# Two transformer blocks on one core: probability transposes in two pairs, and two feed-forward tiles on the un-normed stream

## What is computed

```python
    u = rmsnorm(h, ffn_norm_pre[l])
    gt = causal_dwconv(u @ ffn_w_gate[l], ffn_conv_w[l], ffn_conv_b[l])
    y = (jax.nn.gelu(gt, approximate=True) * (u @ ffn_w_up[l])) @ ffn_w_down[l]
    h = h + rmsnorm(y, ffn_norm_post[l])
```

```python
    logits = scores - slopes * dist.astype(jnp.float32)
    mx = jnp.maximum(logits.max(axis=-1, keepdims=True), sink)
    e = jnp.exp(logits - mx)
    p = e / (e.sum(axis=-1, keepdims=True) + jnp.exp(sink - mx))
    out = jnp.einsum('bkgnqs,bnskd->bnqkgd', p.astype(v.dtype), vv)
```

```python
    s = jnp.einsum('bhtd,bhsd->bhts', q, k) * jnp.exp(log_d - m_t[..., None])
    num = jnp.einsum('bhts,bhsd->bhtd', s, v) + a_inter[..., None] * jnp.einsum('bhtk,bhkv->bhtv', q, c_st)
    c_new = decay[..., None, None] * c_st + jnp.einsum('bhsk,bhsv->bhkv', k * w[..., None], v)
```

## Time and profile before

| | |
|---|---|
| median of 3 runs | 2849.12 us (2843.03 to 2854.50) |
| profiled execution | 2844.58 us, span 2842.8 us |
| granted TensorE clock, mean | 0.974 |
| busy: TensorE, VectorE, ScalarE, GpSimd | 94%, 68%, 45%, 25% |
| way in, way down, mixers | 757 to 1238, 1238 to 1466, 1751 to 1922 us |

### The profile page before, as it was taken

How to read it: one execution, slowest core, us unless ns; L and a number is a source line. 1 busy time by engine, 2 the same in 40 slices (tenths; PEclk the granted TensorE clock), 3 DMA queues, 4 the chain that set the end, 5 groups by cost and what they waited for, 6 DMA issues and landing times. The chain is left out here.

```text
span 2842.8 us, 38460 instructions
## 1 busy us (share of the span) xinstructions
PE 2667.1 (94%) x14346; PEld 2310.5 (81%) x14346; DVE 1919.3 (68%) x2417; ACT 1284.8 (45%) x1968; POOL 711.7 (25%) x446
## 2 busy tenths in 40 slices
PE   8989999999879999999989998889998999999993
PEld 7989999899768888878868887767785688888882
DVE  5366556363388777777884723766355899999996
ACT  4242332332343233234544204764332577777773
POOL 3000000002255555513620000005400244444441
PEclk9999999999989999999999999999998999999997
DMA  5342323343212222266742111114203799999996
GB/s 186 108 133 90 100 97 101 119 138 119 96 45 75 81 89 76 80 216 198 232 140 67 45 60 67 39 45 141 74 18 141 272 422 417 416 415 415 413 413 242
DMA packets 267201, 472.04 MB, mean 166 GB/s; under 512 B 24338, under 2 KB 183330, under 8 KB 241970
## 3 DMA queue, kind: packets, MB, share of 16 engines
q1 hardware_dynamic: 257554, 435.49, 42.8%
q0 software_dynamic: 9504, 34.61, 3.0%
HBM read 398.61 MB, written 71.43 MB: 165 GB/s over the span
## 5 line engine op out<-in xcount | busy, mean ns | idle before, releaser
L4084 DVE TENSOR_TENSOR k_w_lo<-k_raw,k_w_hi 128x2048 fp32r<-128x2048 f32 x192 | 433.4, 2287 | 34.6 <-ACT k_w_hi L4020 31.0
L4020 ACT CAST k_w_hi<-k_raw 128x2048 fp32r<-128x2048 f32 x192 | 363.2, 1912 | 64.3 <-PE bank L3938 41.3
L120 PE MATMUL bank<-u_hi,p_w_hi 128*128 128x342 f32 (+2 forms) x720 | 236.9, 329 | 8.9 <-DVEq L889 6.0
L121 PE MATMUL bank<-u_lo,p_w_hi 128*128 128x342 f32 (+2 forms) x720 | 231.1, 321 | 0.0
L122 PE MATMUL bank<-u_hi,p_w_lo 128*128 128x342 f32 (+2 forms) x720 | 230.8, 321 | 0.0
L3936 PE MATMUL bank<-k_w_hi,k_x_hi 128*128 128x512 f32 x512 | 203.0, 397 | 1.3 <-DVE k_x_lo L4090 1.0
L3938 PE MATMUL bank<-k_w_hi,k_x_lo 128*128 128x512 f32 x512 | 199.8, 390 | 0.0
L3937 PE MATMUL bank<-k_w_lo,k_x_hi 128*128 128x512 f32 x512 | 199.3, 389 | 0.0
L1467 PE MATMUL bank<-u_ffn_hi,f_w_hi 128*128 128x512 f32 (+3 forms) x520 | 170.7, 328 | 16.8 <-DVE f_inner L1757 8.4
L1468 PE MATMUL bank<-u_ffn_lo,f_w_hi 128*128 128x512 f32 (+3 forms) x520 | 167.2, 322 | 0.0
L1469 PE MATMUL bank<-u_ffn_hi,f_w_lo 128*128 128x512 f32 (+3 forms) x520 | 166.7, 321 | 0.0
(11 more groups left out here) (620 smaller groups left out, 7502.7 us busy)
## 6 DMA issues: line engine op xcount, KB each, us to landing
k_raw<-in_w_e_gate_dram SPq DMA_DIRECT2D x64, 1024.0 KB, 7.1
k_raw<-in_w_e_up_dram SPq DMA_DIRECT2D x64, 1024.0 KB, 7.7
k_raw<-in_w_e_down_dram SPq DMA_DIRECT2D x64, 1024.0 KB, 8.3
f_raw<-in_ffn_w_down_dram SPq DMA_DIRECT2D x77, 256.0 KB, 3.0
p_w<-in_w_in_dram SPq DMA_DIRECT2D x34, 512.0 KB, 4.4
f_raw<-inner_scratch SPq DMA_DIRECT2D x55, 256.0 KB, 3.5
f_raw<-in_ffn_w_gate_dram SPq DMA_DIRECT2D x22, 512.0 KB, 3.7
f_raw<-in_ffn_w_up_dram SPq DMA_DIRECT2D x22, 512.0 KB, 4.9
```

Source lines behind the costliest of these rows:

```text
L120: pe.matmul(out, wh[:, t, :], xh[t][:, c:c + n], start=t == 0, stop=False)
L121: pe.matmul(out, wh[:, t, :], xl[t][:, c:c + n], start=False, stop=False)
L4020: act.copy(wh[:, q, :], raw[:, r, :]).then_inc(hi_made, 1)
L4084: dve.tensor_tensor(wl[:, q, :], raw[:, r, :], wh[:, q, :], ALU.subtract).then_inc(lo_made, 1)
```

## The change

*Way in.* Tile 1 also runs on the un-normed stream, right behind tile 0, and its gate and its product are scaled by `token` afterwards; tile 2 is the first on the normed stream and takes its k steps as they come. VectorE makes all low parts of the normed stream and of the sums, GpSimd only those of the weights. Tile 3 becomes a plain tile by columns, and the tiles with seven products begin at 4. TensorE's wait for the first four low weights moves behind the first sums of squares.

```diff
-PLAIN = (0, 1, 2, KF - 1)
+PLAIN = (0, 1, 2, 3, KF - 1)
+FAST_FROM = 4
...
-    GATE = {0: (0, 1, 2), 1: (5, 6, 7), 2: (2, 3, 4), KF - 1: (0, 1, 3)}
-    UP = {0: (3, 4), 1: (0, 1), 2: (5, 6), KF - 1: (4, 5)}
+    GATE = {0: (0, 1, 2), 1: (5, 6, 7), 2: (2, 3, 4), 3: (0, 1, 7), KF - 1: (0, 1, 3)}
+    UP = {0: (3, 4), 1: (0, 1), 2: (5, 6), 3: (5, 6), KF - 1: (4, 5)}
...
             pe.wait_ge(lo_made, 4)
-            for q in (4, 5, 6, 7):
-                low(q)
-            for k in range(2, KD):
-                stream_low(k)
-            low(8)
-            low(9)
-            sums_low(0)
-            low(10)
-            low(11)
-            sums_low(2)
-            for q in range(12, first_operand(KF - 1) + 4):
+            for q in range(4, first_operand(KF - 1) + 4):
                 low(q)
...
+                if n == 1 and k == 0:
+                    pe.wait_ge(g_kept, 1)
                 for j, (c, w) in enumerate(SEQS):
...
+                    if n == 2 and e == 0 and j == 1:
+                        pe.wait_ge(inner_made, 1)
                     for k in range(KD):
+                        if n == 2 and e == 0 and j == 0:
+                            pe.wait_ge(v_lo, k + 1)
...
-            pe.wait_ge(lo_made, 4)
             pe.wait_ge(logs, NL)
...
+                if k == 0:
+                    pe.wait_ge(lo_made, 4)
                 pe.wait_ge(u_lo, k + 1)
                 row_tile(0, k)
             pe.wait_ge(logs2, NL)
             pe.wait_ge(lo_made, 6)
-            pe.wait_ge(g_kept, 1)
             for k in range(KD):
-                if k < 2:
-                    pe.wait_ge(v_lo, k + 1)
-                else:
-                    pe.wait_ge(v_lo2, k - 1)
...
-            pe.wait_ge(g_std, 1)
+            pe.wait_ge(g_kept, 2)
             column_tile(2, 1, SEQS, UP[2], TAPS - 1).then_inc(umm, 1)
+            pe.wait_ge(lo_made, 14)
+            pe.wait_ge(inner_made, 2)
+            column_tile(3, 0, LIVES, GATE[3], 0).then_inc(gmm, 1)
+            pe.wait_ge(lo_made, 16)
+            pe.wait_ge(inner_made, 3)
+            column_tile(3, 1, SEQS, UP[3], TAPS - 1).then_inc(umm, 1)
```

```diff
+    def multiplied(self, engine, step):
+        i, j = divmod(step, HALF_K)
+        if j == HALF_K - 1:
+            engine.wait_ge(self.mm, 4 * (i + 1))
+        else:
+            engine.wait_ge(self.used, (HALF_K - 1) * i + j + 1)
...
                 if j < HALF_K - 1:
                     m.then_inc(d.used, 1)
-                else:
-                    pe.wait_ge(mm, 4 * (i + 1))
-                    pe.sem_inc(d.used, 1)
```

```diff
                 write(i)
+                turn(i, (0, 1))
                 if i < LAST:
                     scores(i + 1, (2, 3))
-                if i == 0:
-                    memory_turn(2)
                 if i:
                     att_sums(i - 1)
-                turn(i)
+                else:
+                    memory_turn(0)
+                turn(i, (2, 3))
                 if i < LAST:
                     keys(i + 1)
                 weigh(i)
+                if i == 0:
+                    memory_turn(1)
                 spread_inverse(i)
                 if i == 0:
-                    memory_turn(3)
+                    memory_turn(2)
                 if i < LAST:
                     decays(i + 1)
...
                 update(i)
+                keep(i)
                 if i < LAST:
                     logits(i + 1, (2, 3))
                 if i == 0:
-                    memory_keep(2)
-                keep(i)
+                    memory_keep(0)
...
-                for g in (0, 2):
+                for g in (0, 1):
                     dve.wait_ge(turned, 4 * n + g + 1)
...
+            decays(0)
+            keys(0)
             exponentials(0, 0)
             exponentials(0, 1)
-            decays(0)
-            keys(0)
```

More of the change, by code:

```diff
@@ L1818, in _ @@
             dve.wait_ge(h_made, KD)
-            stream(0)
-            stream_low(0)
-            dve.wait_ge(gmm, 1)
-            for j, (c, w) in enumerate(LIVES):
-                m = dve.tensor_tensor(g[:, c:c + w], bank[GATE[0][j]][:, 0:w], token[:, c:c + w], ALU.mult)
-            m.then_inc(g_kept, 1)
-            stream(1)
-            stream_low(1)
-            for k in range(2, KD):
-                stream(k)
-            dve.wait_ge(g_kept, 1)
-            conv(0)
+            keep_gate(0)
+            for k in range(4):
+                stream(k)
+            conv(0)
+            stream(4)
+            stream(5)
+            stream_low(0)
+            stream(6)
+            stream_low(1)
+            stream(7)
+            for k in range(2, 5):
+                stream_low(k)
+            multiply(0)
+            for k in range(5, KD):
+                stream_low(k)
+            keep_gate(1)
+            conv(1)
             sums(0)
-            multiply(0)
             sums(1)
-            conv(1)
+            multiply(1)
+            sums_low(0)
             sums_low(1)
+            conv(2)
             sums(2)
-            multiply(1)
+            multiply(2)
             sums(3)
+            sums_low(2)
             sums_low(3)
             for j in range(4):
-                combine(3, j)
-            conv(2)
+                combine(FAST_FROM, j)
+            conv(3)
             for n in FAST:
@@ L2555, in stage_mixers @@
 def stage_mixers(nc, ctx, A, K, bank, qa, ka, va, qk, vm, og, cols, dist, sinks, rows_d, mk, mv, mem_rows, w_in):
-    (scored, logit, maxed, exped, root, turned, pt_kept, pt_kept_odd, pvmm, small, spread, inverse_kept, scaled, sq_made, sums, logs, rstd_made, placed) = sems(
-        ctx, nc, "a", "scored logit maxed exped root turned pt_kept pt_kept_odd pvmm small spread inverse_kept scaled sq_made sums logs rstd_made placed")
+    (scored, logit, maxed, exped, root, turned, pt_kept, pt_kept_late, pvmm, small, spread, inverse_kept, scaled, sq_made, sums, logs, rstd_made, placed) = sems(
+        ctx, nc, "a", "scored logit maxed exped root turned pt_kept pt_kept_late pvmm small spread inverse_kept scaled sq_made sums logs rstd_made placed")
     (bc0, bc1, rm_made, dec, gate_made, fmm, s_made, q_made, kt, kw_made, omm, den_made, hmade, umm, state,
@@ L2716, in write, with turn @@
                 m.then_inc(umm, 1)
-            def turn(n):
-                for g in range(4):
-                    if g == 0 and n:
-                        pe.wait_ge(scaled, n)
-                    if g == 1:
+            def turn(n, groups):
+                for g in groups:
+                    if g == 0:
                         if n:
@@ L2742, in weigh @@
                         probs = pt[:, r, :, :].rearrange("p (g e) t -> p e g t", e=2)[:, kv]
-                        m = pe.matmul(T[1][half, :], va[:, n + r, half], probs, start=r == 0, stop=r == 1)
+                        m = pe.matmul(T[0][half, :], va[:, n + r, half], probs, start=r == 0, stop=r == 1)
                 m.then_inc(pvmm, 1)
@@ L2920, in _ @@
             logits(0, (0, 1))
+            front(0)
+            logits(0, (2, 3))
             maxima(0, 0)
-            logits(0, (2, 3))
-            maxima(0, 1)
-            front(0)
             queries(0)
             weights(0)
+            maxima(0, 1)
             for i in range(NB):
```

182 lines of the change are left out of this document (91 added, 91 removed).

## The result

The changed kernel takes **2822.51 us**, the median of 4 runs (2822.0 to 2826.31); the kernel before, run beside it, 2848.59 (4 runs, 2843.03 to 2854.5). The ratio is 0.9907, with a 95% interval of 0.9887 to 0.9928. The forecast was 2826.5, in a range of 2811 to 2841. The profiled execution took 2822.92 us, with a span of 2821.2: 21.6 less than the span before, where the sum said 22.4.

What follows compares the result with a forecast made beforehand. TensorE, busy 94% of the span, was taken as the limit, VectorE next. Terms 2.0 + 10.3 + 2.9 + 5.3 + 1.6 + 0.3 = 22.4 us took 2844.58 to 2822.2; on the median, 2826.5 us, range 2811 to 2841.

Steps and rivals of the forecast that it cites:

- Way in, start: Feed-forward start: moving TensorE's wait for four low weights shortens ScalarE's 3.12 us wait; 2.0 us won, bounds 0 and 3.1.
- Way in, tiles: Tile 0's end to the first seven-product tile: 77.0 us against 87.3, with a new wait of 6.3; 10.3 us won.
- The point called close: Way in: tile 2's up banks come free near 62 us, wanted at 66, so no wait there.
- Rival (a): Way in stays VectorE's: GpSimd's pieces cost 2.0 each, 4 us lost at tile 2's up banks; 2837 us, chance 0.15.
- Way down: Six product ends cost 0.57 us each, 3.4 together; part given back to VectorE's low rows; 2.9 us won, lower bound 0.
- the sixth: Way down: a sixth of the 3.4 us is given back, because VectorE's low rows are last releaser at a product's end.
- Mixers, period 17.6: Mixers: reads come 17.6 us apart instead of 18.5; 5.3 us won over six periods, bounds 0 and 10.8.
- Gaps under 0.3: Mixers: TensorE's gaps for the probabilities fall under 0.3 us, except the one behind ScalarE's root.
- Rival (b): Mixers don't move: ScalarE's late pair ends too late and its chain keeps the old length; 2833.5 us, chance 0.12.
- Low clock in the mixers: Mixers' last two periods, 20.1 us each with weighing at the low clock: half comes back, 1.6 us won.
- Rival (d): Slower: short waits ahead of every read drop TensorE's clock in the mixers, 10 us a block; 2866 us, chance 0.05.
- First block: Mixers' first block: decays first bring the first read forward by about 3 us; 0.3 us won at the second read.

Runs made afterwards that it cites:

- one swap: Changed kernel with VectorE's second maxima ahead of the memory's second pair and of placing, TensorE's second memory turn ahead of the keys: 2818.14 us.
- the doubled pieces: Changed kernel with GpSimd computing the low halves of weight pieces 6 to 9 twice: 2825.4 us, ratio 0.9905.
- the turns together: Changed kernel with TensorE's four turns of a block's probabilities together again, behind the next block's scores and the square sums: 2837.34 us, ratio 0.9938.
- the mixers alone: Kernel before with only the mixers' part of the change: 2843.80 us, ratio 0.9981.

## Why the prediction was right, and where it was off

- **Way in, start, 2.0:** 2.0 in the pair, 2.1 by the marks inside the stage. ScalarE's wait of 3.12 shrank to 0.56; behind it TensorE waits 0.44 for the second row's low half.
- **Way in, tiles, 10.3:** 12.8 (the first seven-product tile came 74.7 behind tile 0's end, not 77), and 14.1 between the means (three profiles of the old way in, 440.5; seven of the new, 426.4). Tile 1 followed at once, and the wait came where it was put, in two pieces for the low half of the stream. It was 4.1, not 6.3. The term mis-sized was GpSimd's: six pieces at 1.0 were counted, and 5 us were paid, since one piece lay beside an operation that reads PSUM; scalings and low halves counted a shade too long (1.28 for 1.24, 1.2 for 1.15) make some 0.7. Tile 1 took 22.6, not 23.5. The low clock behind the wait went the other way: it cost some 3 us where 2.2 was put. The point called close, tile 2's up banks, held. Rival (a) is out: a piece cost VectorE 1.05 and not 2.0.
- **Way down, 2.9:** 1.3 in the pair of profiles, 2.6 between the means of nine and three. No wait at a product's end is left. The term had two sizes wrong. The six ends cost 3.1, not 3.4: the one shown was among the longer. And VectorE's low rows took back more than the sixth that was put: inside the first and the last product they are waited for 5.5 us in the mean of the nine, against 4.7 in that of the three (leaving out waits of 0.3 and 0.4 at the ends of products that name VectorE), and 6.6 in the first pair. 3.1 less 0.8 is 2.3, near the 2.6.
- **Mixers, period 17.6:** 17.43, but 17.86 for the first of the six, so 6.0 in six periods (111.0, at 18.5 each, less 105.0), not 5.3. The chain was read rightly, down to the wait of ScalarE for the second maxima, which one swap took away. "Gaps under 0.3" was met but for the 0.75 ahead of the keys, which the prediction had placed there, behind ScalarE's root. Rival (b) is out: the period did fall, from 18.5 to 17.43.
- **Low clock in the mixers, 1.6:** it was more, 3.2 in the first pair. With the old order the three profiles show 2, 2 and 4 blocks of 19.7 to 20.3 us; with the new one no block behind the first in nine profiles. The prediction counted half of two blocks; in the new order none is left, which is 2.8 to 6.8 us. Rival (d) is out: with a short wait ahead of every read the clock stayed at 1.00.
- **First block, 0.3:** 1.7 lost in the first pair, 1.3 lost at the same granted clock of 0.85: the sign was wrong. The step "the second maxima now stand behind a memory turn" was right, and worth 2.1. The first read did come forward as put (9.20 us behind the first scores for 12.71), but the block behind it grew by 4.8 at that clock (20.98 to 25.74); beyond the 2.1 what makes it longer was not followed.
- **Outside the sum:** 2.2 us more behind the mixers, where nothing was changed; from profile to profile this stretch varies by 6. The profiled execution before lay 4.0 under its median and the one after at its median, which is where the difference of the medians, 26.1, and that of the spans part. The sum, 22.4, was right for the pair of profiles; 2844.58 less 22.4 plus 4.5 is 2826.7, which the text puts at 2826.5. The median of the changed kernel came 4.2 us below that; its own four runs spread by 4, those of the kernel before by 11.

The sum came out near because errors met: the way in's tiles and the mixers' periods gave 4.8 more than put (2.5 and 2.3), the way down, the first block and the stretch behind the mixers 5.8 less (1.6, 2.0, 2.2). That they met is luck.

## What to carry to other kernels

Walk the limiting engine's list in order, with the neighbour's measured price on each operation that it lengthens: here that gave the new wait within 2.2 us. Then look which operation stands just ahead of the late one. A move on one engine pays through a chain of three: here TensorE's turns came earlier, so VectorE's maxima did, so ScalarE's exponentials did. And before crediting an order with a microsecond, measure between marks inside the stage, and sort the profiles, of both kernels, by TensorE's clock in that stretch.

## What the runs showed of the hardware

**GpSimd and VectorE hold each other up, and not at half speed.** I had read half speed out of the rows before. The rows of the doubled pieces show a beat: each VectorE operation of 1.2 us takes 2.24, and each GpSimd piece 2.1 to 2.3 where one beside PSUM reads takes 1.28. Taken alone that would fit half speed as well as turns by whole instructions. The other case does not fit half speed: with VectorE's low halves back to back, the piece stood for 5.37 us and VectorE lost nothing (six in 6.90). The Trainium skill, page "SBUF — State Buffer", section "SBUF: two separate sides", has an exclusive lock, which a VectorE operation with two SBUF inputs or a GpSimd operation that reads SBUF holds for a whole instruction. The 5.37 beside an unslowed VectorE agrees, and the beat is compatible with it. The price for VectorE is 1.05 a piece and not the 2.0 us that the profile gives for one; that the 2.0 hold the piece's own waiting is the likely reading, and no run separates the two. The same skill, page "Perfetto Trace Analysis", section "Per-instruction lifecycle: what the profiler-reported window actually captures", warns that a GpSimd instruction's reported span is unreliable. Why the pieces alternate in one case and are shut out in the other was not settled.

**TensorE's clock in three orders of the mixers.** The old mixers (TensorE busy 66.63 of 74.00 us at 1.00, before the clock fell) and the order with the turns together (50.61 of 57.35) both fell to a granted 0.92 for two to four blocks; the new order (81.90 of 87.56 in the profile of the mixers alone) did not, behind the first block, in nine profiles. By these rows TensorE was busy 90% and 88% of the time before it fell, and 94% where it did not; whether that decides, or the place of the waits, was not tried. The fall does not come at a fixed block: the old order ran four blocks at 18.5 before it in two profiles and one in the third. In the first block the weighing was at the low clock in five of the nine profiles with the new order, and in none of three with the old, though there other parts of the block were.
